# Two buffers for the convolution's output, another order on VectorE, and loops over layers and blocks written out

## The reference, cut to what matters

```
xa, za = columns of h @ w_in                        # x tile, z tile of a block
x  = conv4(xa) * conv_w + conv_b                    # causal, 4 taps
r, i = sigmoid(x @ w_rg + b_rg), sigmoid(x @ w_ig + b_ig)
a  = exp(-8 * r * softplus(-lam))
u  = sqrt(1 - a*a) * (i * x)
h_t = a_t * h_{t-1} + u_t                           # scan over time
y  = rmsnorm(h) * silu(za)
```

## Time and profile before

| | us |
|---|---|
| median of 3 runs (lowest, highest) | 2710.42 (2710.17, 2716.11) |
| span of the profiled execution, first to last instruction | 2720.3 |
| busy: PE, PEld | 2572.7, 2180.8 |
| busy: DVE, ACT, POOL | 994.4, 818.7, 868.0 |
| chain that ended last, shares | issue 56%, PE 20%, POOL 19% |
| mean granted clock of PE | 0.975 |

### The profile page before, as it was taken

The page is one execution under the profiler, slowest core; times in us unless marked ns, Lnnn a source line. Parts: engine busy times, 40 slices in busy tenths (PEclk is TensorE's granted clock), DMA queues, the critical chain, the costliest instruction groups (busy, mean ns, idle before and its releaser), DMA issues.

```text
span 2720.3 us, 52410 instructions
## 1 busy us (share of the span) xinstructions
PE 2572.7 (95%) x16711; PEld 2180.8 (80%) x16711; DVE 994.4 (37%) x1779; ACT 818.7 (30%) x1546; POOL 868.0 (32%) x651
## 2 busy tenths in 40 slices
PE   7999999999999999879999999999999999996997
PEld 2227879899999989779922388898999999896997
DVE  2241346776111234431103423487731122344113
ACT  0012334444333333322200133344433333333221
POOL 5012224334333333334300232343343333342341
PEclk8999999999999999989999999999999999998999
DMA  8983222223333323234478622232233333222443
GB/s 264 346 287 104 55 57 74 73 71 88 90 90 97 80 75 82 59 110 133 151 239 276 214 72 54 63 81 69 74 98 88 93 85 80 76 68 73 136 125 131
DMA packets 410102, 311.75 MB, mean 115 GB/s; under 512 B 21304, under 2 KB 347840, under 8 KB 408712
## 3 DMA queue, kind: packets, MB, share of 16 engines
q1 hardware_dynamic: 382296, 283.35, 35.8%
q10 hardware_dynamic: 27632, 26.21, 3.1%
HBM read 280.81 MB, written 30.92 MB: 115 GB/s over the span
## 4 chain that ended last, share of the span: by engine, by line
issue 56%; PE 20%; POOL 19%; POOLq 2%; DMA 1%; DVE 0%; SPq 0%; DVEq 0%; ACT 0%; ACTq 0%
POOL w_lo L458 18%; PE misc L513 6%; PE proj L572 4%; PE proj L566 4%; PE proj L568 4%; POOL act_lo L451 1%; POOLq L443 1%; POOLq L441 1%; POOLq L465 1%; POOLq L457 0%; PE misc L521 0%; DMA out_y_prompt<-work 0%; PE misc L489 0%; DVE work L1159 0%; DMA raw<-in_w_in 0%
## 5 line engine op out<-in xcount | busy, mean ns | idle before, releaser
L566 PE MATMUL proj<-act_hi,w_hi 128*128 128x288 f32 (+1 forms) x4672 | 1336.6, 301 | 29.2 <-DVE act_lo L1156 20.1
L568 PE MATMUL proj<-act_lo,w_hi 128*128 128x288 f32 (+1 forms) x4672 | 1312.1, 296 | 0.0
L458 POOL TENSOR_TENSOR w_lo<-raw,w_hi 128x512 fp32r<-128x512 f32 (+1 forms) x584 | 778.4, 1336 | 1432.6 <-ACT w_hi L866 1432.4
L572 PE MATMUL proj<-act_hi,w_lo 128*128 128x288 f32 (+1 forms) x4672 | 1004.1, 296 | 0.0
L566 PEld LDWEIGHTS proj<-act_hi,w_hi 128*128 128x128 f32 (+1 forms) x4672 | 883.1, 189 | 58.8 <-issue 48.0
L568 PEld LDWEIGHTS proj<-act_lo,w_hi 128*128 128x128 f32 (+1 forms) x4672 | 883.6, 189 | 3.4
L572 PEld LDWEIGHTS proj<-act_hi,w_lo 128*128 128x128 f32 (+1 forms) x4672 | 752.3, 188 | 0.0
L866 ACT ACTIVATE w_hi<-raw 128x512 fp32r<-128x512 f32 (+1 forms) x584 | 365.6, 629 | 1186.5 <-PE proj L572 1141.9
L513 PE MATMUL misc<-work,sc 128*2 128x512 f32 x768 | 344.8, 607 | 18.7 <-DMA work<-in_w_ada 11.5
L513 PEld LDWEIGHTS misc<-work,sc 128*2 128x2 f32 x768 | 64.2, 86 | 278.6 <-issue 278.3
L451 POOL TENSOR_TENSOR act_lo<-xy,act_hi 128x576 fp32r<-128x576 f32 x32 | 50.2, 1582 | 352.7 <-ACT act_hi L873 296.2
(11 more groups left out here) (169 smaller groups left out, 1695.0 us busy)
## 6 DMA issues: line engine op xcount, KB each, us to landing
raw<-in_w_in SPq DMA_DIRECT2D x448, 256.0 KB, 2.9
work<-in_w_ada SPq DMA_DIRECT2D x96, 1024.0 KB, 5.2
raw<-in_w_out SPq DMA_DIRECT2D x128, 256.0 KB, 2.8
x_keep<-xy ACTq DMA_DIRECT2D x32, 288.0 KB, 2.5
lb<-x_keep SPq DMA_DIRECT2D x24, 288.0 KB, 3.3
x_keep<-xy ACTq DMA_DIRECT2D x4, 1152.0 KB, 11.6
out_y_prompt<-work SPq DMA_DIRECT2D x4, 1024.0 KB, 3.9
qi_raw<-x_keep SPq DMA_DIRECT2D x8, 288.0 KB, 3.8
```

The lines of the kernel that those rows point to most:

```text
L458: pool.tensor_tensor(w_lo[:, c, :, 0:width], raw[:, c, :, 0:width], w_hi[:, c, :, 0:width].bitcast(F32), ALU.subtract)\
L566: pe.matmul(dst, w_hi[:, c, kk, 0:width], act_hi[:, k, cols], start=(k == 0), stop=False)
L568: pe.matmul(dst, w_hi[:, c, kk, 0:width], act_lo[:, k, cols], start=False, stop=False)
L572: m = pe.matmul(proj[b][0:width, half, 0:HALF], w_lo[:, c, kk, 0:width], act_hi[:, k, cols], start=False, stop=(k == KT - 1))
```

## The change

The convolution's output gets two buffers, `conv_y`: lb[1] for even blocks and the first 584 columns of ki_t for odd ones (the indexer's keys, dead by then; DVE waits for the last indexer score before block 1). DVE's order in a block becomes: two rounds of top-k, convolve(g), recur(g-1), the gate path. ACT's gates(g) wait for the sum of squares of block g-1 (`sq_used`) where they waited for its scans (`hs_ready`). The loops over layers and over the blocks 1 to 7 become Python loops, so that their code stands once for each pass and layer and block numbers are constants; `hold` counts up `ticks` only where its value is still a register's. Loops that stay: modulation blocks, query tiles, output tiles, and POOL's over all tiles.

```diff
--- before.py
+++ after.py
@@ -160,6 +160,7 @@
                  rope[:, :, :].rearrange("p a n -> p (a n)")[:, 0:XC], acc[:, 2 * P:2 * P + XC]]
         g_row = work[:, 0:D_MODEL]
         y_row = [work[:, 2048 + 2048 * j:4096 + 2048 * j] for j in range(2)]
+        conv_y = (lb[1], ki_t[:, 0:584])
         r_x = lb[2][:, 0:T]
         r_b = [lb[n][:, 0:T] for n in (2, 4, 3)]
         z_t = qi_raw
@@ -253,7 +254,8 @@
 
 
             eng.wait_ge(s, value + start[s.name])
-            eng.sem_inc(ticks, 1)
+            if not isinstance(value, int):
+                eng.sem_inc(ticks, 1)
 
         def chunk_no(l, t, c):
             return l * CHUNKS + t * 4 + c
@@ -312,7 +314,7 @@
             ):
                 sp.dma_start(dst, src).then_inc(const_in, 16)
 
-            with sp.Fori(0, DEPTH) as l:
+            for l in range(DEPTH):
 
                 hold(sp, vec_made, l + 1)
                 hold(sp, norm_x, l * 2 * KT)
@@ -361,7 +363,7 @@
                 load(w_in, KI, COL_KI, 80)
                 with sp.Fori(0, 8) as q:
                     load(w_in, QI + q, COL_QI + q * P)
-                with sp.Fori(0, G) as g:
+                for g in range(G):
                     load(w_in, LRU + 2 * g, COL_XA + g * P)
                     load(w_in, LRU + 1 + 2 * g, COL_ZA + g * P)
 
@@ -459,7 +461,7 @@
                                        w_hi[:, c, :, 0:width].bitcast(F32), ALU.subtract)\
                         .then_inc(lo_ready, 1)
 
-            with pool.Fori(0, DEPTH) as l:
+            for l in range(DEPTH):
                 lower(l, 0)
                 split(l, KI, 80)
                 with pool.Fori(1, OUT + 1) as t:
@@ -500,7 +502,7 @@
             pe.wait_ge(xt_read, 20)
             pe.wait_ge(c_ready, 1)
 
-            with pe.Fori(0, DEPTH) as l:
+            for l in range(DEPTH):
 
                 def modulate(j, n):
 
@@ -639,7 +641,8 @@
                     for n, w in enumerate((w_rg, w_ig)):
                         for half in range(2):
                             m = pe.matmul(misc[:, 2 * n + half, 0:WH], w[:, :],
-                                          lb[1][:, half * WH:(half + 1) * WH], start=True, stop=True)
+                                          conv_y[g % 2][:, half * WH:(half + 1) * WH],
+                                          start=True, stop=True)
                     m.then_inc(gates_made, 1)
 
                 def recurrent_block(g, first=False):
@@ -659,7 +662,7 @@
                     chunks(LRU + 1 + 2 * g, 0, g + 5, range(4))
 
                 recurrent_block(0, True)
-                with pe.Fori(1, G) as g:
+                for g in range(1, G):
                     recurrent_block(g)
 
                 def head_side(h, s):
@@ -844,7 +847,7 @@
                     .then_inc(x_kept, 16)
             act.wait_ge(rel_out, 48)
 
-            with act.Fori(0, DEPTH) as l:
+            for l in range(DEPTH):
 
                 hold(act, vec_ready, l + 1)
                 act.activation(sp_[:, 0, :], vec1[:, V1["lam"]:], ACT.Abs)
@@ -952,7 +955,7 @@
                 def gates(g):
 
                     hold(act, gates_made, l * G + g + 1)
-                    hold(act, hs_ready, l * G + g)
+                    hold(act, sq_used, l * SQ_U + g)
                     for n in range(2):
                         act.activation(lb[2 + n][:, 0:W].rearrange("p (a n) -> p a n", a=2),
                                        misc[:, 2 * n:2 * n + 2, 0:WH], ACT.Tanh, scale=0.5,
@@ -989,7 +992,7 @@
 
 
                 recurrent_block(0, True)
-                with act.Fori(1, G) as g:
+                for g in range(1, G):
                     recurrent_block(g)
 
                 def head_side(h, s):
@@ -1200,7 +1203,7 @@
                 dve.reciprocal(dst, dst)
                 dve.drain().then_inc(ms_ready, 1)
 
-            with dve.Fori(0, DEPTH) as l:
+            for l in range(DEPTH):
                 hold(dve, vec_made, l + 2)
                 dve.tensor_copy(vec1[:, :], t_ps[:, 0:P])
                 dve.tensor_copy(vec2[:, :], o_ps[:, 0:48])
@@ -1371,7 +1374,7 @@
                                     .rearrange("p j a -> p (j a)"))
                     hold(dve, evac, l * OUT + LRU + 2 * g + 1)
                     dve.drain()
-                    x, y = lb[0], lb[1][:, 0:W]
+                    x, y = lb[0], conv_y[g % 2][:, 0:W]
                     dve.tensor_copy(stat[:, 0:3, bass.ds(g, 1)].rearrange("p j a -> p (j a)"),
                                     x[:, SEQ:SEQ + 3])
                     dve.tensor_copy(stat[:, 4:7, bass.ds(g, 1)].rearrange("p j a -> p (j a)"),
@@ -1398,7 +1401,8 @@
                 def recur(g):
 
                     hold(dve, root_made, l * G + g + 1)
-                    x, s, ti, t, a = (lb[n][:, 0:W] for n in (1, 2, 3, 4, 5))
+                    x = conv_y[g % 2][:, 0:W]
+                    s, ti, t, a = (lb[n][:, 0:W] for n in (2, 3, 4, 5))
                     stt(s, a, 1.0, s, ALU.add, ALU.mult)
                     stt(t, a, 1.0, t, ALU.add, ALU.mult)
                     stt(ti, ti, 1.0, x, ALU.add, ALU.mult)
@@ -1419,15 +1423,18 @@
                     add_squares(sqb[:, 0, :], l * SQ_U + g)
 
                 def recurrent_block(g, first=False):
+                    for _ in range(2):
+                        best((1, 2, 3), P)
+                    if g == 1:
+
+                        hold(dve, idx_made, (l + 1) * 64)
+                    convolve(g)
                     if not first:
                         recur(g - 1)
-                    convolve(g)
-                    for _ in range(2):
-                        best((1, 2, 3), P)
                     gate_path(LRU + 1 + 2 * g, 0, tile(xy, g))
 
                 recurrent_block(0, True)
-                with dve.Fori(1, G) as g:
+                for g in range(1, G):
                     recurrent_block(g)
 
                 def head_side(h, s):
```

## The result

| | before | after |
|---|---|---|
| median of 4 runs (lowest, highest), us | 2713.27 (2710.17, 2720.56) | 2645.52 (2644.76, 2647.63) |
| ratio, 95% interval | | 0.9746 [0.9729, 0.9762] |
| span of the profiled execution, us | 2720.3 | 2643.0 |
| mean granted clock of PE | 0.975 | 0.985 |
| instructions on the page | 52410 | 45646 |

The changed kernel is 2.5% faster: 67.8 us by the medians, 77.3 by the two profiled spans. The forecast was 2662, and the time lies 6.5 us under the low end of the range.

What follows compares the result with a forecast made beforehand. TensorE, busy 95% of the span, bounds the kernel; only its idle stretches and lower-clock matmuls can be won. 39.6 + 6.8 + 3 = 49.4 us, rounded down to 48, off the median of 2710.42: 2662 us, range 2652 to 2690.

Steps and rivals of the forecast that it cites:

- Part 1: Recurrent stage: two buffers and the new order bring blocks to PE's floor of 27.25 us, gaining 39.6 us in all.
- part 2: Recurrence on DVE: two-SBUF-operand operations and GpSimd subtractions exclude each other, 0.72 against 1.85 us; speaks against a longer DVE chain.
- (a): Recurrent blocks: DVE and GpSimd block each other as often as now; 29.3 us a block, 2686 us; chance 0.11.
- (b): Recurrent blocks: every DVE operation of the convolution is blocked; 32.4 us a block, slower, 2722 us; chance 0.05.
- (d): Recurrent gates: the gap only moves to another wait, for the gates' weights; 2704 us; chance 0.04.
- the missing row of the gates: PE's waits by releaser: sign of a right forecast, no row of gates waiting for the convolution's drain, formerly 24.0 us.
- the twelve waits: Recurrent stage: PE before the gate matmuls waits for the convolution's drain, about 2 us each, 24.0 us in all.
- Part 3: Layer boundary: writing the layer loop out gains 3.36 us idle and some 3.4 of low clock, 6.8 us; bounds 0, 7.3.
- (c): Layer boundary: the gap is not the loop's and stays, part 1 works; 2669 us; chance 0.80 together with the forecast.
- Part 4: Between heads and output tiles: constants for registers and no counts behind waits gain 3 us; bounds 0 and 6.
- the ring: Recurrent blocks: PE's gates, ScalarE's chain, recurrence, convolution, gates again; 30.8 us a block in layer 0, 30.3 in layer 1.

Runs made afterwards that it cites:

- e5: The kernel before with only the two buffers, the new order and ScalarE's new wait, loops and counts kept: 2678.3 us, 0.9857.
- e3: The kernel before with only the loops over the two layers written out, counts, one buffer and old order kept: 2694.45 us, 0.9924.
- e4: The kernel before with the layer loops and the block loops written out, counts, one buffer and old order kept: 2679.7 us, 0.9859.
- e2: The changed kernel with the count back behind every wait, constants or not: 2662.63 us, 0.979.
- e1: The changed kernel with one buffer and the old order, loops written out and no counts behind constant waits: 2650.68 us, 0.9751.
- e11: The changed kernel with two counts behind every wait on all engines: 2698.48 us, 0.9924.

## Why the forecast was off, step by step

**Part 1, right in mechanism and size, and not additive.** Put 0 at PE's start of x tile g as in the forecast. The changed kernel's PE starts one at 434.23 and the next at 461.48, and DVE, ACT and POOL do this (start, duration, idle before):

```profile
434.23 0.29 PE L568 MATMUL proj<-act_hi,w_hi 128*128 128x288 f32 x1
```

```profile
450.84 0.17 DVE L1378 COPY stat<-work 128x3 f32<-128x3 f32 x1 [4.14 <-ACTq L882]
...
452.75 3.49 DVE L1162 SCALAR_TENSOR_TENSOR work<-work,vec 128x580 f32<-128x580 f32 x3
456.36 2.34 DVE L1162 SCALAR_TENSOR_TENSOR lb<-work,lb 128x580 f32<-128x580 f32 x2
458.63 0.75 DVE L1162 SCALAR_TENSOR_TENSOR lb<-lb,ki_t 128x580 f32<-128x580 f32 x1
459.45 0.46 DVE L1410 TENSOR_SCALAR work<-lb 128x580 f32<-128x580 f32 x1
459.83 0.76 DVE L1162 SCALAR_TENSOR_TENSOR lb<-lb 128x580 f32<-128x580 f32 x1
...
461.80 0.33 DVE L1414 TENSOR_TENSOR_SCAN lb<-work,vec,lb 128x64 f32<-128x64 f32 x1
...
466.30 0.76 DVE L1162 SCALAR_TENSOR_TENSOR xy<-qi_raw,proj 128x576 f32<-128x576 f32 x1 [2.31 <-ACTq L953]
```

```profile
462.19 0.63 ACT L975 ACTIVATE sq<-lb 128x512 f32<-128x512 f32 x1 [6.14 <-DVEq L1416]
```

```profile
456.12 1.29 POOL L460 TENSOR_TENSOR w_lo<-raw,w_hi 128x512 fp32r<-128x512 f32 x1 [1.41 <-ACT w_hi L869]
463.84 2.52 POOL L460 TENSOR_TENSOR w_lo<-raw,w_hi 128x512 fp32r<-128x512 f32 x2 [6.43 <-ACT w_hi L869]
```

| us from PE's start of the x tile | forecast | measured |
|---|---|---|
| convolution starts | 16.4 | 16.6 |
| convolution ends | 21.9 | 22.0 |
| scans end | 28.3 | 27.9 |
| x chunk 2 ready (next block) | 4.7 | 4.9 |
| gate path on DVE (next block) | 6.5 | 4.8 |
| period | 27.25 | 27.25 |

Each time is a difference of two rows (450.84 - 434.23; 452.75 + 3.49 - 434.23; 461.80 + 0.33 - 434.23; 463.84 + 2.52 - 461.48, the end of the two subtractions, of which chunk 2 is one; 466.30 - 461.48). Between 457.4 and 463.8 GpSimd does nothing, and the operations that took 1.85, 1.39, 1.84 and 1.31 us take 0.75, 0.46, 0.76 and 0.33. Three of the former are in the earlier trace rows; the second is this row of the kernel before:

```profile
496.34 1.39 DVE L1406 TENSOR_SCALAR work<-lb 128x580 f32<-128x580 f32 x1
```

The rule of part 2 held on both sides: the Trainium skill ("SBUF — State Buffer", section "Who interferes with whom") says that a VectorE instruction with two SBUF inputs contends with a GpSimd instruction that reads SBUF. The trace agrees: with the two engines apart in time, the same operations run in 0.75 us. The tensor_scalar, which reads one tensor, was held up too. The rule did not speak against this order; the order took the collision away. Rivals (a), with 29.3 us a block, and (b), with 32.4, are refuted by the period, and (d) by the missing row of the gates. (By its own terms, 29.3 - 6.2 + 9.1, rival (b) comes to 32.2 us a block; nothing hangs on it.) Beside the 39.6 foreseen, e5 saved 39.6 in the stretches. One reading was too general: behind the twelve waits the clock fell eight times, not always.

But in the changed kernel the same edit is worth some 6 us (6.6 in the stretches). The steps in the two possible series, by the medians' ratios times 2715:

| series 1 | us | series 2 | us |
|---|---|---|---|
| layer loops out (e3) | -20.6 | two buffers, new order (e5) | -38.8 |
| block loops out (e4) | -17.6 | layer and block loops out (e2) | -18.2 |
| constant waits without counts (e1) | -29.3 | constant waits without counts | -12 to -17 |
| two buffers, new order | -1 to -6 | | |

Both end at the same kernel. Three edits shortened one wait, and whichever comes first is credited with it. The forecast put this right in one respect only: it gave the wait to part 1 and did not count it again.

**Part 3, right.** The forecast was 3.36 us idle plus 3.4 of half clock. The changed kernel's first modulation matmul of layer 1:

```profile
1326.77 1.45 PE L515 MATMUL misc<-work,sc 128*2 128x512 f32 x3
```

No idle time stands before it, and the stretch behind it has the clock at 1.00. The loop is the cause: e5, with the layer loop, still has 3.30, and e3, where only the layer loops are gone, has none. Rival (c) is refuted. The kernel before has the loop's branch itself on PE's queue, at the end of each layer (shortest, median and longest in ns). The one at 1359.3, which goes back, takes 5.03 us, the one at 2690.8 takes 0.07. In those 5 us, 1359.3 to 1364.4, the DMA view has one packet on a queue of instructions (packets, MB, share); whose engine's it is, the view does not say:

```profile
L503 PEldq COMPARE_BRANCH  x2: 67/2546/5025, 1359.3 to 2690.8; - x2
```

```profile
q8 instruction: 1, 0.02, 1.4%
```

The Trainium skill's mechanism ("Runtime: NRT & Kernel Launch", section "Instruction fetch mechanics": a taken branch out of the pages held must fetch its target by DMA) agrees with these two rows.

From e5 to e2, in which the layer and block loops go and the counts stay, the two stretches around the boundary shrink by 3.3 and 3.0 us (table below): 6.3 of the 6.8. Against the kernel before, the first of them gained only 1.8 of the 3.4 us of idle time (201.4 to 199.5). The remaining 1.5 us are clock: PE is busy 188.04 us there after the change and 186.04 before, at clock 0.95 and 0.97, and e5, with the loop, has 187.71 at 0.95. Why the clock is lower among the first output tiles there, no run tells.

**Part 4 is the step that failed: "I count some ten hand-overs a layer there at 0.15 us: 1.5 a layer, 3 us. Bounds 0 and 6."** From e5 to the changed kernel, which is parts 3 and 4, the span falls from 2675.8 to 2643.0: 32.8 us. Part 3 as sized takes 6.8 of them, so part 4 is 26 by the profiled spans; by the ratios (0.9857 against 0.9729 to 0.9746) it is 23 to 28. The profiled spans by stretch, each measured from the same landmark to the same landmark in all three (e2's column is that of an execution 5.7 us over its median):

| stretch | e5 | e2 | changed |
|---|---|---|---|
| start to modulation, layer 0 | 30.0 | 28.4 | 27.9 |
| modulation to key tile, layer 0 | 194.5 | 196.6 | 192.6 |
| key tile to first gates, layers 0 and 1 | 387.1 | 382.7 | 378.9 |
| six blocks, twice | 327.0 | 327.0 | 327.0 |
| last head tiles to output, twice | 343.6 | 344.3 | 333.4 |
| output tiles to modulation, layer 1 | 203.0 | 199.7 | 199.5 |
| modulation to key tile, layer 1 | 190.0 | 187.0 | 183.7 |
| the rest: other head tiles, the end | 1000.6 | 1000.5 | 1000.0 |

Three things were wrong in the sizing. The place was right, the last head tiles, but it gave 5 us a layer and not 1.5: the hand-over that e2 and e11 show loses about 0.45 us by one count behind each wait of its chain, where the forecast had 0.15 for counts and registers together. And the forecast priced only idle time, although showed the clock at 0.81 in that very stretch; of the 5.4 us gained there against the kernel before, 2.3 are busy time (157.13 - 154.80) and only 3.0 idle. Second, it was not the only place: the modulation and the key and query tiles, which the forecast did not price, gave another 13 us (1.9 + 8.2 + 6.3, less 3.4 for the clock at the boundary, which is part 3's). Third, "in DVE and ScalarE work that PE covers this is worth nothing" left out the ring, which PE does not cover, as e3 and e4 show; this did not add to the miss, since part 1 had that wait already. How the 26 divides between counts and register work is only known roughly: by the ratios the counts alone are 12 to 17 (e2).

With the measured 26 in place of 3 the sum is 72.4 us, off the span of 2720.3: 2647.9, against 2643.0. Off the median of 2710.42, which the forecast used as its base, it would be 2638.0, 7.5 under the measured 2645.52: the 39.6 and the 26 come from profiled spans, and the profiled execution of the kernel before was 9.9 us over that median. The range failed with it, since the upper bound of 6 was as much of a guess as the value.

## What to carry to other kernels

Price an instruction that every wait brings with it by the number of waits on all engines and by a hand-over that is exposed, and add what the clock costs behind an idle stretch: in the recurrent blocks here it was as much as the idle time that went. When several edits shorten one ring, work out the ring with the cheap ones already done: the reordering was worth 39 us on the kernel before and 6 on the kernel with constants and without counts. Where the ring is longer than the busiest engine, register work and counts on the other engines are on the path.

## What the runs showed that was not expected

- An instruction more behind a wait costs 5 to 8 us a thousand in this kernel: 2336 of them 12 to 19 us, another 4668 of them 36. In the first step they are the waits themselves, which without the count are carried by the instruction behind; in the second they are counts alone. Both cost about the same, though the profile gives one only 51 ns on PE, 17 on ScalarE and 21 on DVE.
- Over a third of the win is no idle time: 32.3 of 77.3 us are busy time of the same matmuls, most of it by the higher granted clock. Waits of 0.3 to 1.2 us once a block left the clock at 1.00 in all 24 blocks of e1 and e4. Of the twelve waits of 2.0 us in the kernel before, four left it there; right behind the other eight it fell, which cost 1.7 us more each.
- Writing out the loops over two layers alone gave 12.0 us in the recurrent blocks (366.6 to 354.6), though the block loop and its register g were still there. Five blocks fewer ran with the lower clock; waiting went down by only 3.3 us.
- PE's 27.25 us a block is not fixed. Layer 0 of e11 did the same six blocks without idle time, at the same granted clock, 1.2% faster than layer 1; why, no run tells:

```profile
425.07:586.59 161.52, 161.52 (x1202) 158.85 (x1201) 116.93 (x228) 76.01 (x123) 62.87 (x46) 1.00 0.31 83
1738.05:1901.53 163.48, 163.48 (x1203) 160.82 (x1201) 116.99 (x228) 76.47 (x124) 61.92 (x47) 1.00 0.31 82
```
